# Five block ends of a two-layer float32 model: products of the first token half issued ahead, loads and remainders in other orders, and half-width increments in a triangular inverse

## The chip, the cores and the metric

The kernel runs on one core of one Trainium2 chip. The metric is the device time of one execution in microseconds (us), as the median of the runs. The profile is of one more execution; its times are us from its first instruction. Engines are written as the profile writes them: PE is the matrix engine (PEld its weight loads), DVE the vector engine, ACT the scalar engine, POOL GpSimd, SP the queue that issues the DMAs.

## What is computed

The reference is one block of a conformer kind, then two blocks with a memory attention each, all on 256 tokens of width 1024 in float32:

```
x = first_block(x, c, ...)          # conformer convolution, then conv_ffn (D_FF 2816)
for layer in (0, 1):
    x = layer_norm(ALPHA * x + 0.5 * swiglu(x, ffn1...))
    # layer 0: rwkv7_mix, a recurrence over tokens; layer 1: stick_breaking_mix
    x = layer_norm(ALPHA * x + mixer(x @ w_in) @ w_out)
    x = layer_norm(ALPHA * x + 0.5 * swiglu(x, ffn2...))
```

The recurrence is `state = state * w_t - (state kk_t) b_t^T + v_t k_t^T`, with a 64 x 64 state for each of 12 heads. The kernel solves it by chunks of 64 tokens, which needs the inverse of a triangular 64 x 64 matrix for each head and chunk.

## The kernel before

**Products.** Every matrix is held as two parts of type float32r, a rounded one (index 0, "hi") and the remainder (index 1, "lo"), and a product is three matmuls, hi x hi, hi x lo and lo x hi (`mm3`, lines 145 to 147). Tokens stand on the moving side: `actT[:, part, k, :]` holds the transposed activations, 8 tiles k of 128 features by 256 tokens. A weight tile of 128 x 128 is stationary. `FIRST` is the token half 0 to 127, `SECOND` the half 128 to 255.

**Weights.** Chunks of weights arrive by DMA in two raw buffers in turn (`Ring.load`, issued in order on SP). ACT rounds a chunk (`split_hi`), DVE or POOL makes the remainder (`split_lo`), and PE waits for `lo_done`. A raw buffer is loaded again only when `lo_done` has counted the remainder of the chunk in it, and a pair of parts is written again only when PE has used it.

**Order.** Each engine's order is written out by hand, stage after stage; the semaphores alone order the engines among each other. The stages are `ffn_stage` for the first block's FFN (`conv=True`) and four more, `rwkv_stages` (projections) and `rwkv_core`, and `stick_stages`.

**A block's end.** The last products of a stage are done by token half and column half (`BLOCKS`). `norm_dve_side` and `norm_act_side` normalize half 0 while PE works on half 1. PE turns half 0 (`turn_tokens(pe, hand, 0)`), and ACT and DVE make its hi and lo parts: `token_hi[0]` counts the six tiles of ACT, `token_lo[0]` first DVE's two tiles. `keep_busy(n)` issues n matmuls of the identity with itself, in plain float32, whose results nobody reads. After the last products come `keep_busy(pe, 14)`, and in the next stage the turning of half 1, `keep_busy(pe, 4)`, and `first_products`: for every k the two products of the hi tokens, then for every k the lo tokens' product (line 474). It has two outputs (gate and up) in the three FFN stages that follow a normalization, and one in `rwkv_stages` and `stick_stages`. That makes five such starts. `tokens_act` and `tokens_dve` make the parts of half 1; `pair_hi` counts the tiles 0, 1 and 2, 3 that DVE rounds, `token_hi[1]` the tiles 4 to 7 of ACT.

**The inverse.** `rwkv_core` does two rounds (T = 0, 1), each for two chunks and two groups p of six heads. It starts from a block diagonal of width 2, and level l (1 to 5) doubles the blocks. `squares` is 12 matmuls of 64 x 64 x 64 in plain float32, 6 heads by 2 chunks. A level computes Z = M D, the increments D Z and Z D^T into banks 2 + p and 4 + p, and DVE adds each whole bank to `Dm` or `DT` (lines 2652 and 2655).

Of the kernel before, what the change touches and what calls it, by code (L numbers as in the profile page):

```python
# [23 lines left out]
ALU = mybir.AluOpType  # L24
# [200 lines left out]
def build_program(nc, A, out):  # L225
    with ExitStack() as ctx:
# [179 lines left out]
        def tokens_dve(dve, i, t, yb, norm):  # L406

            w = slice(t * P, (t + 1) * P)
            dve.wait_ge(token_turned[t], 2 * i + 1)
# [7 lines left out]
            dve.wait_ge(token_hi[0], i + 1)  # L417
            first_lo(dve, yb, ACT_COLS).then_inc(token_lo[0], 1)
# [37 lines left out]
        def first_products(pe, i, outs, weights):  # L456

            for k in range(KD):
                if k == 0:
                    pe.wait_ge(token_hi[0], i + 1)  # L460
                    pe.wait_ge(token_lo[0], 2 * i + 2)
                    pe.wait_ge(pair_hi, 2 * i - 1)
                elif k == 2:
                    pe.wait_ge(pair_hi, 2 * i)
                elif k == 4:
                    pe.wait_ge(token_hi[1], i + 2)
                for n, out_ in enumerate(outs):
                    w = weights(n, k)
                    pe.matmul(out_, w[0], actT[:, 0, k], start=k == 0, stop=False)  # L469
                    pe.matmul(out_, w[1], actT[:, 0, k], start=False, stop=False)  # L470
            for k in range(KD):
                wait_tokens(pe, k, i)
                for n, out_ in enumerate(outs):
                    ins = pe.matmul(out_, weights(n, k)[0], actT[:, 1, k], start=False, stop=k == KD - 1)  # L474
            return ins

# [8 lines left out]
        FIRST = slice(0, P)  # L485
# [33 lines left out]
        SECOND = slice(P, 2 * P)  # L519
# [32 lines left out]
        def first_block():  # L552
# [135 lines left out]
            with nc.Block() as block:  # L688
                @block.sync
                def _(sp):  # L690
                    sp.dma_start(x_tok, A["x"][0].rearrange("(t p) d -> p t d", p=P)).then_inc(x_loaded, 16)
                    sp.dma_start(par[:, 0:n_first], A["par"][:, 0:n_first]).then_inc(params_loaded, 16)
                    for u in range(4):
                        for i in unit_chunks(u):
# [10 lines left out]
                    sp.dma_start(mem_raw.rearrange("p (k m) -> p k m", k=KD),  # L705
                                 A["mem_2"].rearrange("(k p) m -> p k m", p=P)).then_inc(mem_loaded, 16)
# [5 lines left out]
                    ring_a.load(sp, g_cols + 4)  # L712
                    sp.dma_start(rows[:, 0], A["norm_post_mix"][0].partition_broadcast(P)).then_inc(gates_loaded, 16)
# [3 lines left out]
                    load_mod(sp, 16)  # L717
                    load_mod(sp, 17)
# [549 lines left out]
        def ffn_stage(name, conv, norm, hand, next_a, next_b, take):  # L1268
# [202 lines left out]

            def up_first(pe):

                gate, up = ps[:, 4, 0:SEQ], up_of(0, 0)
                weights = lambda n, k: [a_parts[:, 0, s, n * BCH + k * P:n * BCH + (k + 1) * P] for s in range(2)]
                if conv:
                    ins = input_products(pe, gate, up, weights)
                else:
                    pe.wait_ge(ring_a.lo_done, sa + 1)
                    ins = first_products(pe, got, [gate, up], weights)  # L1480
                ins.then_inc(ring_a.used, 1)
# [375 lines left out]
        def rwkv_stages(take):  # L1857
# [88 lines left out]
            def _(pe):  # L1946
                def project(c):
# [6 lines left out]
                    if c == 0:  # L1954
                        first_products(pe, got, [chunk_bank(c)[:, 0]], lambda n, k: [
                            ring_a.part(g0, s, k * P, k * P + P) for s in range(2)]).then_inc(ring_a.used, 1)
                        return
# [12 lines left out]

                turn_tokens(pe, got, 1)
# [42 lines left out]
            def _(act):  # L2014
# [75 lines left out]
            def _(dve):  # L2090
# [84 lines left out]
        def rwkv_core(R, K, V, Q, BB, BON, CUM, KK, lowg, g_up, w_end, level_mask, pair_mask, below, upto, ident2,  # L2175
# [43 lines left out]
            def bank(b):  # L2219
                return ps[:, b, 0:H6 * HD].rearrange("p (m t) -> p m t", m=H6)  # L2220

# [81 lines left out]
            def _(pe):  # L2303
# [30 lines left out]

                for T in range(NT):
# [11 lines left out]
                    for l in LV:  # L2347
# [20 lines left out]
                        for p in range(2):  # L2368
# [213 lines left out]
            def _(dve):  # L2582
# [45 lines left out]
                for T in range(NT):  # L2628
# [19 lines left out]
                    for l in LV:  # L2648
                        for p in range(2):
                            if l < 5:  # L2650
                                dve.wait_ge(pe_out.sem, pe_out.at((("dD", l), T, p)))
                                dve.tensor_tensor(Dm[:, p], Dm[:, p], bank(2 + p), ALU.add)\
                                    .then_inc(dve_out.up((("D", l), T, p)), 1)
                            dve.wait_ge(pe_out.sem, pe_out.at((("dDT", l), T, p)))
                            dve.tensor_tensor(DT[:, p], DT[:, p], bank(4 + p), ALU.add)\
# [63 lines left out]
        def stick_stages(take, hand, got_norm):  # L2719
# [61 lines left out]
            def _(pe):  # L2781
                def project(c, n):
                    g = g0 + c
                    if c == 0 and n == 0:
                        return first_products(pe, got, [ps[:, bank(c), 0:SEQ]], lambda n, k: [
                            ring_a.part(g, s, k * 256, k * 256 + P) for s in range(2)])
# [80 lines left out]

                turn_tokens(pe, got, 1)
# [251 lines left out]
```

## Time and profile before

| what | value |
|---|---|
| median of 3 runs | 1456.42 us (1456.1 to 1458.33) |
| the profiled execution's own time | 1456.55 us |
| its span, first to last instruction | 1454.8 us |
| mean granted clock of PE in it | 0.998 of full speed |
| PE busy | 1414.5 us, 97% of the span |
| PEld busy | 1290.6 us, 89% |
| DVE busy | 952.5 us, 65% |
| ACT busy | 683.7 us, 47% |
| POOL busy | 156.9 us, 11% |

Matmuls overlap, and a row's duration holds the whole way through the array, so a matmul of 280 ns may follow another by less than half of that. What counts is the distance from start to start. A row of a timeline may stand for several instructions of one kind (x24): its length goes from the first one's start to the last one's end.

### The profile page before, as it was taken

The page shows a single profiled execution, that of the slowest core. Times are in us where ns is not written, and L with a number is a line of the kernel's source. Part 1 is how long each engine was busy: PE and PEld are TensorE (multiplying, and loading weights), DVE is VectorE, ACT ScalarE, POOL GpSimd, SP SyncE. Part 2 cuts the span into 40 slices and gives each one's busy share as a digit, 9 for nine tenths or more (in the row PEclk, how much of TensorE's full clock was granted, in tenths as well). Part 3 has the DMA queues.
Part 4 walks back from the last instruction along what each step waited for, and adds up shares of the span by engine and source line. Part 5 has one row for each costly group of instructions (what it writes and reads, how often), then busy time and mean ns, then how long its engine had stood idle before and what let it go on. Part 6 is the DMA issues. An engine that isn't in the chain of part 4 may idle for free.

```text
span 1454.8 us, 31311 instructions
## 1 busy us (share of the span) xinstructions
PE 1414.5 (97%) x12733; PEld 1290.6 (89%) x12733; DVE 952.5 (65%) x1290; ACT 683.7 (47%) x880; POOL 156.9 (11%) x182
## 2 busy tenths in 40 slices
PE   6999999999999999999989999999999999999997
PEld 5868799999999998988879999999999898899996
DVE  3657786667655556795786655675656778855656
ACT  5455654455433436743435433454334476534332
POOL 1442033221000004021300000000000011000000
PEclk9999999999999999999999999999999999999999
DMA  8975566666666645321036666566666344576662
GB/s 349 355 291 203 158 210 183 189 196 177 175 188 184 191 143 183 116 89 61 4 113 201 180 187 195 166 202 188 187 189 186 125 139 162 158 218 183 187 190 85
DMA packets 293910, 257.76 MB, mean 177 GB/s; under 512 B 7104, under 2 KB 270272, under 8 KB 290752
## 3 DMA queue, kind: packets, MB, share of 16 engines
q1 hardware_dynamic: 293824, 256.49, 57.5%
q8 instruction: 68, 1.11, 0.3%
q14 instruction: 18, 0.15, 0.0%
HBM read 255.42 MB, written 1.05 MB: 176 GB/s over the span
## 4 chain that ended last, share of the span: by engine, by line
PE 50%; DVE 4%; ACT 1%; issue 0%; DVEq 0%; ACTq 0%
PE ps L145 14%; PE ps L146 14%; PE ps L147 14%; PE ps L2331 3%; PE ps L383 1%; DVE stats L342 1%; DVE arena L340 1%; PE ps L390 1%; PE ps L469 0%; PE ps L474 0%; PE ps L470 0%; PE ps L2314 0%; PE ps L2322 0%; DVE gate_m L2634 0%; PE ps L2817 0%
## 5 line engine op out<-in xcount | busy, mean ns | idle before, releaser
L145 PE MATMUL ps<-actT,a_parts 128*128 128x256 f32 x2096 | 588.3, 281 | 2.9 <-DVE a_parts L130 2.0
L146 PE MATMUL ps<-actT,a_parts 128*128 128x256 f32 x2096 | 585.0, 279 | 0.0
L147 PE MATMUL ps<-actT,a_parts 128*128 128x256 f32 x2096 | 584.9, 279 | 0.0
L145 PEld LDWEIGHTS ps<-actT,a_parts 128*128 128x128 f32 x2096 | 394.0, 188 | 12.1 <-issue 3.8
L146 PEld LDWEIGHTS ps<-actT,a_parts 128*128 128x128 f32 x2096 | 393.8, 188 | 4.2
L147 PEld LDWEIGHTS ps<-actT,a_parts 128*128 128x128 f32 x2096 | 393.9, 188 | 0.0
L1350 DVE TENSOR_TENSOR a_parts<-a_raw,a_parts 128x2048 fp32r<-128x2048 f32 x100 | 238.4, 2384 | 54.5 <-ACT a_parts L1347 54.1
L1364 DVE TENSOR_TENSOR b_parts<-b_raw,b_parts 128x1024 fp32r<-128x1024 f32 x72 | 88.3, 1226 | 160.3 <-ACT b_parts L1361 160.3
L1347 ACT ACTIVATE a_parts<-a_raw 128x2048 fp32r<-128x2048 f32 x100 | 190.4, 1904 | 0.8 <-DMA a_raw<-in_ffn_w_up 0.8
L1361 ACT ACTIVATE b_parts<-b_raw 128x1024 fp32r<-128x1024 f32 x90 | 95.3, 1058 | 171.0 <-PE ps L147 171.0
L145 PE MATMUL ps<-b_parts,hid 128*128 128x512 f32 x400 | 158.1, 395 | 1.0 <-DVE hid L1461 1.0
L146 PE MATMUL ps<-b_parts,hid 128*128 128x512 f32 x400 | 158.3, 396 | 0.0
L147 PE MATMUL ps<-b_parts,hid 128*128 128x512 f32 x400 | 158.3, 396 | 0.0
L1409 ACT ACTIVATE arena<-ps 128x256 f32<-128x256 f32 x88 | 33.8, 385 | 241.6 <-PE ps L147 241.5
L130 DVE TENSOR_TENSOR a_parts<-a_raw,a_parts 128x2048 fp32r<-128x2048 f32 (+2 forms) x38 | 81.3, 2139 | 43.8 <-ACT a_parts L125 43.7
L147 PEld LDWEIGHTS ps<-b_parts,hid 128*128 128x128 f32 x400 | 75.1, 188 | 18.2
L1455 DVE TENSOR_TENSOR arena<-arena,ps 128x256 f32<-128x256 f32 x88 | 37.0, 421 | 81.3 <-ACT arena L1409 81.3
L145 PEld LDWEIGHTS ps<-b_parts,hid 128*128 128x128 f32 x400 | 75.1, 188 | 15.1 <-POOL b_parts L130 1.2
L146 PEld LDWEIGHTS ps<-b_parts,hid 128*128 128x128 f32 x400 | 75.1, 188 | 13.8
L125 ACT ACTIVATE a_parts<-a_raw 128x2048 fp32r<-128x2048 f32 (+2 forms) x43 | 77.0, 1791 | 14.7 <-DMA a_raw<-in_a_pw_w 11.8
L1364 POOL TENSOR_TENSOR b_parts<-b_raw,b_parts 128x1024 fp32r<-128x1024 f32 x18 | 45.9, 2547 | 107.6 <-ACT b_parts L1361 107.6
L1461 DVE TENSOR_TENSOR hid<-arena,hid 128x256 fp32r<-128x256 f32 x110 | 46.8, 426 | 3.8
(392 smaller groups left out, 1818.8 us busy)
## 6 DMA issues: line engine op xcount, KB each, us to landing
a_raw<-in_ffn_w_gate SPq DMA_DIRECT2D x88, 512.0 KB, 4.0
a_raw<-in_ffn_w_up SPq DMA_DIRECT2D x88, 512.0 KB, 5.2
b_raw<-in_ffn_w_down SPq DMA_DIRECT2D x88, 512.0 KB, 3.3
arena<-in_mod_w SPq DMA_DIRECT2D x24, 1024.0 KB, 10.1
a_raw<-in_f_up_w SPq DMA_DIRECT2D x44, 512.0 KB, 5.0
b_raw<-in_f_down_w SPq DMA_DIRECT2D x22, 512.0 KB, 3.3
a_raw<-in_rwkv_w_in SPq DMA_DIRECT2D x10, 1024.0 KB, 5.3
a_raw<-in_sb_w_in SPq DMA_DIRECT2D x10, 1024.0 KB, 5.1
```

The lines of the kernel that those rows point to most:

```text
L125: act.activation(self.parts[:, g % 2, 0, w], self.raw[:, g % 2, w], ACT.Copy).then_inc(self.hi_done, 1)
L130: dve.tensor_tensor(self.parts[:, g % 2, 1, w], self.raw[:, g % 2, w], self.parts[:, g % 2, 0, w].bitcast(F32), ALU.subtract).then_inc(sel ...
L145: pe.matmul(out, lhs[0], rhs[0], start=start, stop=False)
L146: pe.matmul(out, lhs[0], rhs[1], start=False, stop=False)
L147: return pe.matmul(out, lhs[1], rhs[0], start=False, stop=stop)
L1347: act.activation(a_parts[:, q, 0], a_raw[:, q], ACT.Copy).then_inc(ring_a.hi_done, 1)
L1350: dve.tensor_tensor(a_parts[:, q, 1], a_raw[:, q], a_parts[:, q, 0].bitcast(F32), ALU.subtract).then_inc(ring_a.lo_done, 1)
L1361: act.activation(b_of(q, j)[:, 0], b_raw[:, q], ACT.Copy).then_inc(ring_b.hi_done, 1)
L1364: lo.tensor_tensor(b_of(q, j)[:, 1], b_raw[:, q], b_of(q, j)[:, 0].bitcast(F32), ALU.subtract).then_inc(ring_b.lo_done, 1)
L1455: dve.tensor_tensor(hf[:, q], cg[:, q], up, ALU.mult).then_inc(f_step, 1)
L1461: dve.tensor_tensor(h_of(q, j)[:, 1], hf[:, q], h_of(q, j)[:, 0].bitcast(F32), ALU.subtract).then_inc(h_done, 1)
L2331: ins = pe.matmul(bank(b)[half[c], mm], lhs[half[c], p, mm], rhs[half[c], p, mm], start=True, stop=True)
```

## The change

1. `first_ahead` is new. It issues the hi tokens' two products of half `FIRST` alone for one output, 16 matmuls with 128 moving columns. It stands ahead of `turn_tokens(pe, got, 1)` for the one output of `rwkv_stages` and `stick_stages` (the change's own title speaks of four block ends; the code has five such starts), and in the FFN stages for the gate ahead of the turning and for the up projection behind it, in place of `keep_busy(pe, 4)`. `first_products` then does only `SECOND` for the hi tokens; its lo tokens' products stay 256 wide. `tokens_dve` makes the lo part of half 0's six tiles before it waits for the turned half 1.
2. Four orders: the load of `mem_2` in the first block goes behind the 17th chunk of `mod_w`, and chunks 17 and 18 go ahead of four loads of rows; POOL's second remainder at the start of the first FFN waits for DVE's remainder of a weight chunk; ACT rounds chunk 2 of the recurrent stage ahead of `take_out(0)`; DVE makes the remainders of chunks 1 and 2 ahead of the `k_a` and `mu` columns and of `mix(0)`.
3. In the inverse, `one_side` computes 32 of the 64 columns of each increment (those of the even blocks for `Dm`, of the odd ones for `DT`; the others are zero) into a packed bank, and DVE adds 192 elements in place of 384.

```diff
@@ tokens_dve
+            dve.wait_ge(token_hi[0], i + 1)
+            first_lo(dve, yb, ACT_COLS).then_inc(token_lo[0], 1)
             dve.wait_ge(token_turned[t], 2 * i + 1)
...
-            dve.wait_ge(token_hi[0], i + 1)
-            first_lo(dve, yb, ACT_COLS).then_inc(token_lo[0], 1)
@@ first_products
-                    pe.wait_ge(token_hi[0], i + 1)
-                    pe.wait_ge(token_lo[0], 2 * i + 2)
...
-                    pe.matmul(out_, w[0], actT[:, 0, k], start=k == 0, stop=False)
-                    pe.matmul(out_, w[1], actT[:, 0, k], start=False, stop=False)
+                    for part in w:
+                        pe.matmul(out_[:, SECOND], part, actT[:, 0, k, SECOND], start=False, stop=False,
+                                  skip_group_check=True)
...
+        def first_ahead(pe, i, n, out_, weights):
+
+            for k in range(KD):
+                if k == 0:
+                    pe.wait_ge(token_hi[0], i + 1)
+                    pe.wait_ge(token_lo[0], 2 * i + 2)
+                for s, part in enumerate(weights(n, k)):
+                    pe.matmul(out_[:, FIRST], part, actT[:, 0, k, FIRST], start=k == 0 and s == 0, stop=False,
+                              skip_group_check=True)
@@ first block, SP
-                    sp.dma_start(mem_raw.rearrange("p (k m) -> p k m", k=KD),
-                                 A["mem_2"].rearrange("(k p) m -> p k m", p=P)).then_inc(mem_loaded, 16)
                     load_mod(sp, 12)
...
                     ring_a.load(sp, g_cols + 4)
+                    load_mod(sp, 16)
+                    sp.dma_start(mem_raw.rearrange("p (k m) -> p k m", k=KD),
+                                 A["mem_2"].rearrange("(k p) m -> p k m", p=P)).then_inc(mem_loaded, 16)
+                    load_mod(sp, 17)
...
-                    load_mod(sp, 16)
-                    load_mod(sp, 17)
@@ ffn_stage, PE
-                if take is not None:
+                if take is not None and got_norm is not None:
+                    pe.wait_ge(ring_a.lo_done, sa + 1)
+                    first_ahead(pe, got, 0, first_outs[0], first_weights)
                     turn_tokens(pe, got, 1)
-                    keep_busy(pe, 4 if got_norm is not None else 5)
+                    first_ahead(pe, got, 1, first_outs[1], first_weights)
+                elif take is not None:
+                    turn_tokens(pe, got, 1)
+                    keep_busy(pe, 5)
@@ ffn_stage, POOL, first FFN only
                     ring_b.split_lo(pool, gb)
+                    pool.wait_ge(ring_a.lo_done, ga + 3)
                     ring_b.split_lo(pool, gb + 1)
@@ rwkv_stages, PE; in stick_stages the output is ps[:, bank(0), 0:SEQ]
+                ring_a.wait_split(pe, g0)
+                first_ahead(pe, got, 0, chunk_bank(0)[:, 0], first_weights)
                 turn_tokens(pe, got, 1)
                 keep_busy(pe, 4)
@@ rwkv_stages, ACT
                 next_hi(1)
+                next_hi(2)
                 act.wait_ge(dve_out.sem, dve_out.at("mu"))
                 take_out(0)
-                next_hi(2)
@@ rwkv_stages, DVE
                 take[1](dve)
+                next_lo(1)
...
-                next_lo(1)
+                next_lo(2)
                 mix(0)
-                next_lo(2)
                 mix(1)
@@ rwkv_core
+            def side(ap, l, odd):
+                return ap.rearrange("q (g two w) -> q g two w", two=2, w=1 << l)[:, :, odd]
...
+                def one_side(p, b, lhs, rhs, l, odd):
+                    for mm in range(H6):
+                        out_ = packed_bank(b)[:, mm * HD // 2:(mm + 1) * HD // 2]
+                        for c in range(2):
+                            ins = pe.matmul(packed(out_[half[c]], l), lhs[half[c], p, mm],
+                                            side(rhs[half[c], p, mm], l, odd), start=True, stop=True)
+                    return ins
...
-                                squares(p, 2 + p, DT, Z).then_inc(pe_out.up((("dD", l), T, p)), 1)
-                            squares(p, 4 + p, Z, DT).then_inc(pe_out.up((("dDT", l), T, p)), 1)
+                                one_side(p, 2 + p, DT, Z, l, 0).then_inc(pe_out.up((("dD", l), T, p)), 1)
+                            one_side(p, 4 + p, Z, DT, l, 1).then_inc(pe_out.up((("dDT", l), T, p)), 1)
...
-                                dve.tensor_tensor(Dm[:, p], Dm[:, p], bank(2 + p), ALU.add)\
+                                even = side(all_heads(Dm[:, p]), l, 0)
+                                dve.tensor_tensor(even, even, packed(packed_bank(2 + p), l), ALU.add)\
```

## Rows read from the trace of the kernel before

**Rows 1.** The core's span and mean granted PE clock.
```profile
core 0: 1454.8 us, clock 0.998
```

**Rows 2.** PE's waits over the whole span: us in total, times, longest.
```profile
PE ps L619 <- DMA arena<-in_mod_w: 2.2, 2, 1.2
...
PE ps L145 <- DVE a_parts L130: 2.0, 3, 1.2
...
PE ps L2380 <- DVE gate_f L2655: 1.5, 2, 0.8
...
PE ps L145 <- DVE hid L1461: 1.0, 1, 1.0
...
PE ps L2331 <- DVE gate_m L2652: 0.7, 1, 0.7
...
PE ps L2308 <- DVE arena L2604: 0.5, 1, 0.5
```

**Rows 3.** PE's timeline where `("ffn1", 1)` starts: start, us, engine, line.
```profile
954.02 3.29 PE L383 MATMUL ps<-ident 128*128 128x128 f32 x28
957.14 1.06 PE L390 MATMUL ps<-ident,x_tok 128*128 128x128 f32 x8
...
962.82 2.03 PE L474 MATMUL ps<-actT,a_parts 128*128 128x256 f32 x16
964.69 0.28 PE L145 MATMUL ps<-actT,a_parts 128*128 128x256 f32 x1
```

**Rows 4.** Timeline of ACT and DVE at the same place.
```profile
955.07 0.84 ACT L499 ACTIVATE actT<-arena 128x768 fp32r<-128x768 f32 x1
...
955.80 0.37 DVE L490 TENSOR_TENSOR actT<-arena,actT 128x256 fp32r<-128x256 f32 x1
...
959.54 0.29 DVE L416 CAST actT<-arena 128x256 fp32r<-128x256 f32 x1
...
959.78 0.63 ACT L404 ACTIVATE actT<-arena 128x512 fp32r<-128x512 f32 x1
```

**Rows 5.** PEld's timeline in `rwkv_stages`, around 24 matmuls with 2 moving columns.
```profile
594.37 2.76 PEld L1988 LDWEIGHTS ps<-head_ones,arena 128*128 128x128 f32 x24
597.05 0.19 PEld L145 LDWEIGHTS ps<-actT,a_parts 128*128 128x128 f32 x1
```

**Rows 6.** PEld's group of the token transposes: busy, mean ns.
```profile
L390 PEld LDWEIGHTS ps<-ident,x_tok 128*128 128x128 f32 x96 | 10.3, 141 | 5.3 <-DVE x_tok L365 4.5 <-DVE x_tok L1724 0.6
```

**Rows 7.** Timelines of ACT and PE at the start of `rwkv_stages`.
```profile
558.18 0.63 ACT L404 ACTIVATE actT<-arena 128x512 fp32r<-128x512 f32 x1
...
561.26 0.47 ACT L2022 ACTIVATE arena<-ps,small 128x256 f32<-128x256 f32 x1 [1.49 <-PE ps L474]
...
561.71 0.39 PE L145 MATMUL ps<-actT,a_parts 128*128 128x256 f32 x1 [0.55 <-DVE a_parts L130]
...
565.95 0.39 PE L145 MATMUL ps<-actT,a_parts 128*128 128x256 f32 x1 [1.17 <-DVE a_parts L130]
```

**Rows 8.** PE's timeline at the start of `stick_stages`.
```profile
1152.61 1.25 PE L474 MATMUL ps<-actT,a_parts 128*128 128x256 f32 x8
```

**Rows 9.** PE's timeline in a level of the inverse, then two DVE groups by shape.
```profile
664.86 1.57 PE L2331 MATMUL ps<-gate_m,arena 64*64 64x64 f32 x48
...
L2655 DVE TENSOR_TENSOR gate_f<-gate_f,ps 128x384 f32<-128x384 f32 x20 | 11.1, 553 | 8.0 <-PE ps L2331 6.0
...
L1455 DVE TENSOR_TENSOR arena<-arena,ps 128x256 f32<-128x256 f32 x88 | 37.0, 421 | 81.3 <-ACT arena L1409 81.3
```

**Rows 10.** Timelines of POOL and DVE at the start of the first FFN.
```profile
181.72 4.99 POOL L130 TENSOR_TENSOR b_parts<-b_raw,b_parts 128x1024 fp32r<-128x1024 f32 x2 [62.86 <-DVE a_parts L1387]
...
184.49 2.38 DVE L1459 CAST hid<-arena 128x256 fp32r<-128x256 f32 x1
```

**Rows 11.** Timelines of SP and ACT in the first block, `mem_2`'s load and first reader.
```profile
52.90 4.07 SPq L705 DMA_DIRECT2D b_raw<-in_mem  x1
...
102.37 1.90 ACT L853 ACTIVATE b_parts<-b_raw 128x2048 fp32r<-128x2048 f32 x1
```

More of the change, by code:

```diff
@@ L473, in first_products @@
                 for n, out_ in enumerate(outs):
-                    ins = pe.matmul(out_, weights(n, k)[0], actT[:, 1, k], start=False, stop=k == KD - 1)
-            return ins
+                    ins = pe.matmul(out_, weights(n, k)[0], actT[:, 1, k], start=False, stop=k == KD - 1,
+                                    skip_group_check=True)
+            return ins
+        def first_ahead(pe, i, n, out_, weights):
[5 more added lines that the diff above has]
+                    pe.matmul(out_[:, FIRST], part, actT[:, 0, k, FIRST], start=k == 0 and s == 0, stop=False,
+                              skip_group_check=True)
         def first_affine(eng, i, yb, norm, ks, scaled):
@@ L483, in first_affine @@
             return ins
-        FIRST = slice(0, P)
+        FIRST, SECOND = slice(0, P), slice(P, 2 * P)
         ACT_COLS, DVE_COLS = slice(0, 6), slice(6, KD)
@@ L1470, in up_of, with first_weights @@
                 return ps[:, 1, SEQ:2 * SEQ] if kicked(q, j) else ps[:, 4 + q, SEQ:2 * SEQ]
+            first_outs = [ps[:, 4, 0:SEQ], up_of(0, 0)]
+            def first_weights(n, k):
+                return [a_parts[:, 0, s, n * BCH + k * P:n * BCH + (k + 1) * P] for s in range(2)]
             def up_first(pe):
-                gate, up = ps[:, 4, 0:SEQ], up_of(0, 0)
-                weights = lambda n, k: [a_parts[:, 0, s, n * BCH + k * P:n * BCH + (k + 1) * P] for s in range(2)]
                 if conv:
-                    ins = input_products(pe, gate, up, weights)
+                    ins = input_products(pe, *first_outs, first_weights)
                 else:
-                    pe.wait_ge(ring_a.lo_done, sa + 1)
-                    ins = first_products(pe, got, [gate, up], weights)
+                    ins = first_products(pe, got, first_outs, first_weights)
                 ins.then_inc(ring_a.used, 1)
@@ L1954, in project @@
                     if c == 0:
-                        first_products(pe, got, [chunk_bank(c)[:, 0]], lambda n, k: [
-                            ring_a.part(g0, s, k * P, k * P + P) for s in range(2)]).then_inc(ring_a.used, 1)
+                        first_products(pe, got, [chunk_bank(c)[:, 0]], first_weights).then_inc(ring_a.used, 1)
                         return
@@ L1969, in low_rank, with first_weights @@
                     ins.then_inc(norm_pe.up(name), 1)
+                def first_weights(n, k):
+                    return [ring_a.part(g0, s, k * P, k * P + P) for s in range(2)]
+                ring_a.wait_split(pe, g0)
+                first_ahead(pe, got, 0, chunk_bank(0)[:, 0], first_weights)
                 turn_tokens(pe, got, 1)
@@ L2220, in bank, with packed, all_heads, packed_bank @@
                 return ps[:, b, 0:H6 * HD].rearrange("p (m t) -> p m t", m=H6)
+            def side(ap, l, odd):
+                return ap.rearrange("q (g two w) -> q g two w", two=2, w=1 << l)[:, :, odd]
+            def packed(ap, l):
+                return ap.rearrange("q (g w) -> q g w", w=1 << l)
+            def all_heads(ap):
+                return ap.rearrange("q m t -> q (m t)")
+            def packed_bank(b):
+                return ps[:, b, 0:H6 * HD // 2]
             def bmask(m):
@@ L2784, in project @@
                     if c == 0 and n == 0:
-                        return first_products(pe, got, [ps[:, bank(c), 0:SEQ]], lambda n, k: [
-                            ring_a.part(g, s, k * 256, k * 256 + P) for s in range(2)])
+                        return first_products(pe, got, [ps[:, bank(c), 0:SEQ]], first_weights)
                     for k in range(KD):
@@ L2866, in behind, with first_weights @@
                         turn(4)
+                def first_weights(n, k):
+                    return [ring_a.part(g0, s, k * 256, k * 256 + P) for s in range(2)]
+                ring_a.wait_split(pe, g0)
+                first_ahead(pe, got, 0, ps[:, bank(0), 0:SEQ], first_weights)
                 turn_tokens(pe, got, 1)
```

4 lines of the change are left out of this document (2 added, 2 removed).

## The prediction

> **What bounds the kernel.** I read the cores view first: a span of 1454.8 us at a mean granted clock of 0.998 [rows 1], so nothing here is about the clock. The profiled execution took 1456.55 us, 1.75 around its span and 0.13 above the median of the three runs, and the sum is made against 1456.55. Then the page: PE is busy for 97% of the span, so a change gains where it takes matmuls from PE or ends one of PE's waits. The waits view says how little there is of the second kind [rows 2]: 2.0 us for remainders made by DVE, 1.5 and 0.7 and 0.5 us in the inverse, 1.0 us for `hid`. Last come the timelines at the edited places, where the distances from start to start tell what a matmul costs.
>
> **Products of half 0 ahead.** In the FFN stage of [rows 3] PE turns half 1 at 957.14, does `keep_busy(4)`, 32 hi products and 16 lo products of 256 columns, and begins the next tile at 964.69. That is 8 transposes, 8 instructions of `keep_busy` and 48 products, 64 slots in 7.55 us: 0.117 each (the 16 of line 474 take 1.87 us, 0.117 each). `keep_busy(14)` keeps its place, so PE is free for the new products at 957.14 and no sooner. What they wait for is then there: ACT's six tiles are done at 955.91 and DVE's lo tiles at 956.17 [rows 4].
>
> The new order counts: 16 half products, 8 transposes, 16 half products, 32 half products of `SECOND`, 16 lo products 256 wide. 32 full products and 8 fillers go, 64 half ones come. With h for a half product the stretch takes 64 h + 24 x 0.117 = 64 h + 2.80, against 64 x 0.117 = 7.47. All hangs on h, and no float32r matmul of the trace moves fewer than 256 columns. The nearest row is line 1988: 24 matmuls with 128 x 128 weights and only 2 moving columns. Their loads begin at 594.37 and the next load at 597.05 [rows 5], so each takes 0.112 us though almost nothing moves. The weight load sets the pace. A half product loads the same 128 x 128 weights as a whole one, and the change loads every hi and lo weight tile twice. I take h = 0.112, with 0.117 (the whole product's) above.
>
> Nothing behind it is late. With h = 0.112 the turning moves 1.8 us later, DVE's second pair from 959.83 to 961.6 and ACT's four tiles from 960.41 to 962.2 [rows 4]. PE would begin `SECOND` at 957.14 + 1.79 + 0.93 + 1.79 = 961.65 and want k = 4 at 963.4. The lo part of half 0's six tiles, moved ahead of DVE's wait, runs in the time in which DVE waits for the later turning. So each of the three FFN starts costs 7.15 + 2.80 - 7.47 = +2.5 us, together **+7.5** (+7.0 at 0.109, +8.4 at 0.117).
>
> The Trainium skill speaks for another h here. "TensorE: Matmul & The Clock Gate", section "Back-to-back issue gap", gives about 81 ns for a matmul with its weight load at 128 columns. By it the three starts would cost 3 x (64 x 0.081 + 2.80 - 7.47) = +1.5 us. The row of line 1988 shows 112 ns for the load alone, so I leave the rule among the rivals.
>
> In `rwkv_stages` one output gets 16 half products ahead, 1.79 us, and its 16 hi products become half ones. ACT's tiles come at 558.81 + 1.79 = 560.60 [rows 7] and hold k = 4. Then 8 half and 8 whole products end at 562.45, 1.6 us after 560.85 (561.26 less the 0.41 in which ACT sees it). The next chunk's rounding, at 561.63 behind `take_out(0)`, now goes first: it starts at about 562.85, 1.2 later. PE waited for that chunk's remainder until 565.95 and will wait until 567.15: **+1.2** (0.9 to 1.4). The order of ACT and DVE is thus worth the 0.4 us that it takes off 1.6. `take_out(0)`, `mix(0)` and the tanh behind them come some 2 us later, hidden by the 5.6 us of the third chunk's products; without that cover the low-rank products would be late by it.
>
> In `stick_stages` ACT's tiles hold k = 4 too. Before, the 8 lo products began at 1152.61 [rows 8]; ACT's tiles move by 1.79, and half products save 0.1 to 0.2 of it behind k = 4: **+1.6** (1.4 to 1.9). Five starts: 7.5 + 1.2 + 1.6 = +10.3.
>
> **The inverse.** 48 instructions of `squares` take 1.57 us less one matmul's 0.22 from first to last start, 0.029 each, so 24 (12 matmuls of two passes) 0.70 [rows 9]. Two chunks run side by side, so a pair takes 0.058, half of 0.117 with half of the 128 weight columns. The weights stay 64 x 64. By the proportion of lines 1988 and 145, 0.112 to 0.117, the pair falls to 0.056. There are 4 + 5 calls for two groups and two rounds, 36 of them, with 12 pairs each: 432 x 0.0025 = -1.1. The other bound is that the moving columns set the pace: -432 x 0.029 = -12.5. Above, nothing.
>
> DVE's additions hide behind PE, except at four places: two waits for the last `DT`, one for `Dm` at level 1 of round 1, one behind `DT` ahead of the normalization [rows 2]. An addition of 384 elements takes 0.553 and one of 256 takes 0.421 [rows 9], so 192 take 0.355, 0.2 less: -0.8. The stepped access has no row. Every addition but these four has PE's 0.7 us a call as cover, so a slower one costs at most that 0.8. Together **-1.9** (0 to -13.3).
>
> **POOL at the first FFN.** POOL makes two remainders in one stretch, 181.72 to 186.71, and a cast of DVE that begins in it, 128 x 256, takes 2.38 us [rows 10] where the same shape elsewhere takes 0.29 [rows 4]. It ends with POOL's. PE waits 1.0 us for `hid` behind it [rows 2]. With the second remainder held until DVE's chunk, the cast is done in 0.3 us and the wait goes: **-1.0** (0 to -1.1). The held remainder starts about 188. PE wants it only after the first remainder's products and another tile's, and SP's load behind it, some 1 us later than now, is for the tile after that.
>
> **Loads in the first block.** PE waits for a load twice and only for `mod_w` [rows 2], both times ahead of the moved ones. `mem_2` is issued at 52.90 and first read at 102.37 [rows 11]. SP now stops at chunk 17 of `mod_w`, until PE has used a slot, ahead of `mem_2` and the four rows. PE uses that slot in the products of the third of eight tiles, and `mem_2` is read in the fifth and the rows from the fifth on. **0** (-0.5 to +0.5).
>
> **Sum.** 1456.55 + 10.3 - 1.9 - 1.0 = 1463.95, say **1464.0 us**, 0.5% slower.
>
> **Rivals.** *Half products cost by their columns.* Line 390's loads of 128 columns take 141 ns where others take 188 [rows 6], so a load need not take 112. If h falls to 0.058, an FFN stretch is 64 x 0.058 + 2.80 - 7.47 = -1.0, given back in part by a wait of about 0.5 for ACT's four tiles: -1.4 over three, 0.2 for the other two starts. The time is 1456.55 - 1.2 - 1.9 - 1.0 = 1452.4, faster. All terms balance at 256 h - 18.5 = 2.9, h = 0.084. Against it stand 24 loads at 0.112. In between, at h = 0.081, I get +3.3 - 2.9, 1456.9. That h is the figure of the Trainium skill's section above.
>
> *The increments pay by their columns.* -12.5 for -1.1 in the inverse gives 1452.6, faster too. For it: 64 columns in two passes and 64 weight columns could each be the limit of a pair. Against it the same row of 2 columns.
>
> *A narrow float32r product runs as a plain float32 one.* `keep_busy(14)` is 28 instructions in 3.12 us [rows 3]: a plain product of 128 columns costs two, 0.23. Then 256 h - 18.5 = +41, 1494.7. For it: no narrow one stands in the trace. Against it: nothing does but that float32r is one instruction wherever it stands.
>
> *The orders of loads do more than hold.* A late row or a late `mem_2` would stop PE near 102 us; 1 to 5 us more, 1466 to 1469.
>
> **Chances.** The forecast's case 0.64. Half products by columns or nearly so 0.12, half of it below 1453.5. Increments by columns 0.07. Plain float32 pace 0.11. Loads late 0.03; another mix, near no change, 0.03. A measurement of this kernel tells about 0.2%, 2.9 us, from no change. Below 1453.5 lie 0.06 + 0.06; within lie the rest of the second rival, and a twelfth of the first case where the inverse gives back 5 or more: 0.15; slower 0.73. The range that leaves out the plain pace and the fastest ends is 1455 to 1468.
>
> **What would show it.** In the changed kernel's timeline, `first_ahead` has 16 products in 1.8 us and `SECOND` the same pace as before; the next tile of the `("ffn1", 1)` start begins 10.0 us after the end of `keep_busy(14)`. The x24 rows of the increments still lie 0.67 to 0.70 apart, DVE's additions take 0.36, and the cast at the first FFN takes 0.29 with PE's wait for `hid` gone. The prediction is wrong if the new products lie 0.06 or 0.23 apart, or if the increments' calls shrink to 0.4 us.

## The result, and the profile after

The changed kernel takes 1466.17 us (median of 6 runs, 1464.62 to 1467.32). The kernel before, run beside it, takes 1458.34 (6 runs, 1456.1 to 1458.78). The ratio is 1.0058, 95% interval [1.0048, 1.0069]: slower by 0.6%. The prediction said 1464.0, slower by 0.5%, range 1455 to 1468.

The profiled execution of the changed kernel has a span of 1463.7 us, 8.9 more than [rows 1]. The cores view of it:

```profile
core 0: 1463.7 us, clock 0.998
```

PE's timeline at the start of `("ffn1", 1)`, answering [rows 3] (`first_ahead` is line 484, `SECOND` 468, the lo products 473):

```profile
956.66 3.29 PE L383 MATMUL ps<-ident 128*128 128x128 f32 x28
959.70 1.98 PE L484 MATMUL ps<-actT,a_parts 128*128 128x128 f32 x16
961.52 1.06 PE L390 MATMUL ps<-ident,x_tok 128*128 128x128 f32 x8
962.34 1.98 PE L484 MATMUL ps<-actT,a_parts 128*128 128x128 f32 x16
964.15 3.74 PE L468 MATMUL ps<-actT,a_parts 128*128 128x128 f32 x32
967.73 2.10 PE L473 MATMUL ps<-actT,a_parts 128*128 128x256 f32 x16
969.67 0.28 PE L145 MATMUL ps<-actT,a_parts 128*128 128x256 f32 x1
```

From start to start the half products take (961.52 - 959.70) / 16 = 0.114 us ahead, with the hand-over to the turning in it, and 3.58 / 32 = 0.112 in `SECOND`. A whole product took 0.117 [rows 3]. Half the columns save 4% of the time. No wait stands between the rows: PE is full from 956.66 to 969.67, 13.01 us. Before, the same stretch ran from 954.02 to 964.69 [rows 3], 10.67. The difference is +2.34.

DVE there, answering [rows 4]:

```profile
959.61 0.95 DVE L500 TENSOR_TENSOR actT<-arena,actT 128x768 fp32r<-128x768 f32 x1
962.18 0.73 DVE L415 TENSOR_SCALAR arena<-ps,par 128x128 f32<-128x128 f32 x2 [1.62 <-PE ps L390]
962.95 0.29 DVE L418 CAST actT<-arena 128x256 fp32r<-128x256 f32 x1
```

The moved lo part ends at 960.56, inside the time in which DVE waits for the later turning. The first pair is there at 963.24 (962.95 + 0.29), 0.9 us before PE wants it for `SECOND` at 964.15.

The start of `rwkv_stages`, answering [rows 7], and of `stick_stages`, answering [rows 8]:

```profile
559.16 1.69 PE L468 MATMUL ps<-actT,a_parts 128*128 128x128 f32 x12 [0.24 <-DVE actT L418]
...
566.23 0.39 PE L145 MATMUL ps<-actT,a_parts 128*128 128x256 f32 x1 [1.21 <-DVE a_parts L130]
```
```profile
1157.73 1.68 PE L468 MATMUL ps<-actT,a_parts 128*128 128x128 f32 x12 [0.24 <-DVE actT L418]
```

With one output and not two, PE waits 0.24 us for DVE's pair, a wait that the prediction didn't name. It is hardly new: the kernel before waits 0.17 us for the same pair, at 558.29 and at 1150.98. The second chunk's remainder lets PE go on at 566.23, where it did at 565.95 [rows 7]; but by then the kernel is 0.86 us ahead of the old one (the gain in the first FFN, below), so this start costs 0.28 + 0.86 = +1.1.

The inverse, answering [rows 9]. Two neighbouring rows of PE's timeline, then DVE's additions by shape between 640 and 740 us:

```profile
662.58 0.87 PE L2373 MATMUL ps<-gate_f,arena 64*64 64x32 f32 x24
663.28 0.87 PE L2373 MATMUL ps<-arena,gate_f 64*64 64x32 f32 x24
```
```profile
L2699 DVE TENSOR_TENSOR gate_f<-gate_f,ps 128x192 f32<-128x192 f32 x20 | 7.1, 353 | 11.4 <-PE ps L2373 11.4
L2695 DVE TENSOR_TENSOR gate_m<-gate_m,ps 128x192 f32<-128x192 f32 x16 | 5.6, 352 | 12.9 <-PE ps L2373 12.9
```

24 instructions of 32 moving columns still lie 0.70 us apart: PE gains nothing by the missing columns. DVE's additions fell from 0.553 to 0.353, and the stepped access costs nothing. PE's waits, answering [rows 2]:

```profile
PE ps L2355 <- issue: 2.3, 3, 1.5
...
PE ps L2422 <- DVE gate_f L2699: 1.1, 2, 0.6
...
PE ps L2364 <- DVE gate_m L2695: 0.5, 1, 0.5
...
PE ps L2341 <- DVE arena L2646: 0.3, 1, 0.3
```

Three of the inverse's waits are 0.8 us shorter in all, and the one for `hid` (1.0 before) is gone. New is 2.3 us of "issue", in which PE waited for nothing that the profile shows; the kernel before had 0.4 on that line. The longest, 1.5 us near 646, is in the profiles of all four kernels that have the products ahead (1.2 to 1.6) and of none without. It costs next to nothing: in the others PE waits 0.9 us right behind that place, for the DVE operation that is line 2634 in the kernel before, and in these four that wait is gone.

DVE and POOL at the first FFN, answering [rows 10]:

```profile
184.37 0.30 DVE L1468 CAST hid<-arena 128x256 fp32r<-128x256 f32 x1
...
191.14 2.59 DVE L1470 TENSOR_TENSOR hid<-arena,hid 128x256 fp32r<-128x256 f32 x1
```
```profile
188.09 2.41 POOL L130 TENSOR_TENSOR b_parts<-b_raw,b_parts 128x1024 fp32r<-128x1024 f32 x1 [4.12 <-DVE a_parts L1359]
191.05 2.40 POOL L1373 TENSOR_TENSOR b_parts<-b_raw,b_parts 128x1024 fp32r<-128x1024 f32 x1 [0.55 <-ACT b_parts L1370]
```

The cast fell from 2.38 to 0.30 us. The collision isn't gone, only moved: a remainder of DVE, 0.43 elsewhere, now takes 2.59 beside POOL's at 191.05, where PE doesn't wait for it. In both kernels the held instruction ends 0.2 to 0.3 us behind POOL's (186.87 and 186.71, 193.73 and 193.45). The Trainium skill has the rule, on its page "SBUF — State Buffer", section "Who interferes with whom": a cast in DVE's two-port mode, or a `tensor_tensor` with both inputs in SBUF, shares a port pair with GpSimd, and whoever comes second is held for the other's whole instruction. The two held durations agree with it; that the cast runs in the two-port mode, no row shows.

Holding POOL's remainder back has a price that the prediction put at nothing. SP issues its loads in order, and the load of `b_raw` that waits for this remainder is now issued at 190.68, not 186.89. The two loads of `a_raw` behind it are late by 2.0 us. First the row of the kernel before, then those of the changed kernel:

```profile
189.71 1.00 SPq L1318 DMA_DIRECT2D a_raw<-in_f_up_w  x2
```
```profile
191.70 1.00 SPq L1327 DMA_DIRECT2D a_raw<-in_f_up_w  x2
192.56 1.92 ACT L1356 ACTIVATE a_parts<-a_raw 128x2048 fp32r<-128x2048 f32 x1 [1.59 <-DMA a_raw<-in_f_up_w]
206.15 0.38 PE L145 MATMUL ps<-actT,a_parts 128*128 128x256 f32 x1 [0.21 <-DVE a_parts L1359]
```

ACT waits 1.59 us for that load, its rounding and then DVE's remainders come later, and PE waits 0.21 us where it did not wait before. From start to start the early `hid` gains 1.2 us, and 0.4 to 0.5 of it is lost again here. Six profiles have POOL's new wait. In two of them ACT waits 0.76 and 1.06 us for this load and PE not at all; in four ACT waits 1.56, 1.59, 1.61 and 1.86 and PE 0.17, 0.21, 0.23 and 0.50. Why the load lands sooner in some is open.

### The profile page after: what moved, and what is told of

It reads as the page before. It is cut to its first block, busy times and chain, and to the rows that moved or that the text cites. A ratio compares the mean times of both kernels' runs of the same rounds, so it can differ in the third digit from the quotient of the medians.

```text
span 1463.7 us, 31520 instructions
## 1 busy us (share of the span) xinstructions
PE 1426.0 (97%) x12837; PEld 1302.4 (89%) x12837; DVE 945.6 (65%) x1290; ACT 683.4 (47%) x880; POOL 156.7 (11%) x182
## 4 chain that ended last, share of the span: by engine, by line
PE 51%; DVE 4%; issue 1%; ACT 0%; DVEq 0%; ACTq 0%
PE ps L145 14%; PE ps L146 14%; PE ps L147 14%; PE ps L2373 2%; PE ps L2364 1%; PE ps L383 1%; PE ps L468 1%; PE ps L484 1%; DVE stats L342 1%; DVE arena L340 1%; PE ps L390 1%; PE ps L2355 0%; PE ps L473 0%; PE ps L2347 0%; PE ps L2860 0%
```

## Where the clock fell

The totals of two profiles can't be compared to 1 us here until one thing is taken out. At one place in `rwkv_stages` and at one at the end of the recurrence's round 1 the granted clock falls to 0.50 (1.2 GHz) for 3 to 4 us in some profiles and not in others, with the same instructions. Two windows tables of PE (stretch, its length, PE busy, instructions, clock, DMA share and GB/s), first of the kernel with only the new order of loads, then of the one with only the narrow increments:

```profile
597.00:598.00 1.00, 1.00 (x11) 0.99 1.09 388
598.00:599.00 1.00, 1.00 (x7) 0.50 0.93 312
599.00:600.00 1.00, 1.00 (x7) 0.50 0.00 0
```
```profile
597.00:598.00 1.00, 1.00 (x10) 1.00 1.10 392
598.00:600.00 2.00, 2.00 (x20) 1.00 0.37 124
```

What PE did just before is the same in both: 24 matmuls that move 2 columns each, 2.7 us. The second place comes behind 64 x 64 products with a wait of 1.34 us between them, and the changed kernel's own profile has it:

```profile
732.00:734.00 2.00, 1.41 (x35) 0.79 1.15 350
734.00:736.00 2.00, 2.00 (x41) 0.50 0.73 289
```

Cut at five landmarks of PE's timeline, all profiles become comparable. Columns: from `keep_busy(14)` at the start of `rwkv_stages` to the 24 two-column matmuls; on to the memory scores; on to the 12 products with `g_up` in round 1; on to the second turning for the norm; the last four columns are from one turning of half 0 to the next across the starts of `ffn2`/0, `ffn1`/1, `stick_stages`, and the last start with what lies behind it to the span's end. * is a stretch in which the clock fell.

```
                 start   scores   inverse  end of   start of  start of  start of  last start
                 rwkv                      round 1  ffn2,0    ffn1,1    stick     to end
before           42.06   16.71    113.77   19.03    191.10    191.08    110.92    201.1
changed          43.31   16.71    113.04   19.63*   193.47    193.46    112.39    203.5
inverse only     42.15   16.71    112.45   19.92*   191.08    191.08    110.93    201.1
no ahead         41.77   16.71    112.40   19.87*   191.21    191.09    110.84    201.1
ahead only       43.72   18.27*   113.79   19.62*   193.47    193.47    112.39    203.5
pool only        42.17   18.21*   114.03   19.00    191.09    191.09    110.92    201.1
gate behind      42.17   18.25*   114.10   19.82*   191.75    191.74    110.77    201.8
rwkv order only  41.78   18.24*   113.73   19.01    191.09    191.18    110.87    201.2
loads only       42.17   18.25*   114.02   18.98    191.09    191.09    110.86    201.2
```

The first fall costs 1.54 us (18.25 less 16.71), the second 0.6 to 0.9. The profile of before has neither, and its execution is 1.8 us below the median (1456.55 against 1458.34). The Trainium skill ("TensorE: Matmul & The Clock Gate", section "Seeing it yourself") calls clock events in a trace not fully reliable; here the instruction counts agree with them, 7 matmuls to the microsecond in place of 10 or 11.

## The experiments

Each kernel below is the kernel before with the edit named, unless it says otherwise. Ratios are to the kernel before on the same chip.

**The parts by themselves.** Four kernels: (1) only `one_side` and its additions; (2) all of the change but the products ahead; (3) only the products ahead, with `first_lo` moved; (4) only POOL's wait. The core of (2) against the changed kernel:

```diff
-                if take is not None and got_norm is not None:
-                    pe.wait_ge(ring_a.lo_done, sa + 1)
-                    first_ahead(pe, got, 0, first_outs[0], first_weights)
+                if take is not None:
                     turn_tokens(pe, got, 1)
-                    first_ahead(pe, got, 1, first_outs[1], first_weights)
-                elif take is not None:
-                    turn_tokens(pe, got, 1)
-                    keep_busy(pe, 5)
+                    keep_busy(pe, 4 if got_norm is not None else 5)
```

(1) 

> The kernel before with only the narrow increments of the inverse. My theory, with what the trace after has shown: the pairs keep their 0.058 us, so PE gains nothing per call; DVE's shorter additions end four waits sooner, worth 0.5 to 1.9 us in all: 0.9987 to 1.0 of before. Rival, pay by moving columns: 12 us less (0.992). Rival, the change costs here: stepped access or new waits on DVE make it 1 us or more slower.

(2) 

> The changed kernel without its products ahead at the block ends: inverse, POOL's wait, the orders of loads and the rwkv orders stay. My theory: the products ahead are the whole loss, so this is 1.5 to 3.5 us faster than before (0.9976 to 0.999) and some 10 us faster than the changed kernel. Rival, the cost is shared or sits in the orders: no faster than before.

(3) 

> The kernel before with only the products ahead at the five starts. My theory: 64 half products at 0.112 us in each FFN start, 2.5 us each, 1.6 in rwkv_stages (where its old orders stay) and 1.6 in stick_stages: +10 to +11 us, 1.007 of before. Rival, half products pay by columns: -1 us, 0.999. Rival, plain float32 pace: +41 us, 1.028.

(4) 

> The kernel before with only POOL's wait ahead of its second remainder. My theory: the cast takes 0.3 us in place of 2.4 and PE's 1 us wait for hid goes: 0.7 to 1.1 us less, 0.9993 of before, at the edge of what the measurement tells; its trace shows the wait gone. Rival: the remainder, moved later, blocks another operation that PE waits for, and the time is the same or more.

```
                 median    ratio    95% interval       span of the profile
inverse only     1457.18   0.9995   [0.9987, 1.0004]   1454.5
no ahead         1455.44   0.9989   [0.9980, 0.9998]   1452.8
ahead only       1467.18   1.0066   [1.0053, 1.0079]   1467.0
pool only        1457.07   1.0000   [0.9991, 1.0008]   1456.2
```

The products ahead are the whole loss: alone they cost 0.66%, and without them the rest is faster than before. (1) and (4) are too small for the timing; the traces carry them. In the table above the inverse stretch is 113.73 to 114.10 with wide increments and 112.40 or 112.45 in (1) and (2): 1.3 to 1.7 us gained. In (4) PE's wait for `hid` is gone, and from its wait at 175 us to the turning at 360 it needs 0.75 us less than before: 1.2 gained, and 0.4 lost again where it waits 0.17 us for DVE's remainder at 206.56, as the changed kernel does. So the rival stated for (4), that another operation comes late, is true in part. In (2) that wait is missing, and the same stretch takes 1.3 us less. The rival that the half products pay by columns would have made (3) 0.999.

**How many slots, or how late?** The products ahead do two things: more matmuls and a later turning. Call a slot the place of one matmul instruction on PE; a start has 64 before. This kernel separates them. It has half products for the gate alone, at the three FFN starts alone, and behind the turning where the fillers were:

```diff
-                if take is not None:
+                if take is not None and got_norm is not None:
                     turn_tokens(pe, got, 1)
-                    keep_busy(pe, 4 if got_norm is not None else 5)
+                    pe.wait_ge(ring_a.lo_done, sa + 1)
+                    first_ahead(pe, got, 0, first_outs[0], first_weights)
+                elif take is not None:
+                    turn_tokens(pe, got, 1)
+                    keep_busy(pe, 5)
```

> The kernel before with the half products of the gate alone, at the three FFN starts alone, and behind the turning in place of the four fillers, so that nothing is turned later. PE then has 8 transposes, 32 half and 32 whole products where it had 64 slots. My theory, cost by count: 32 x 0.112 + 40 x 0.117 - 7.47 = +0.8 us each, +2.4 in all (1.0016). Rival, cost by columns: -0.9 each, -2.8 in all (0.998). Rival, the loss comes from the later turning and not from the count: no change or better.

1459.11 us, ratio 1.0014 [1.0005, 1.0023]; by the table 0.66 us for each start (191.75 less 191.09), 2.0 in all. Its timeline:

```profile
960.38 1.06 PE L390 MATMUL ps<-ident,x_tok 128*128 128x128 f32 x8
961.20 1.98 PE L490 MATMUL ps<-actT,a_parts 128*128 128x128 f32 x16
963.01 0.39 PE L471 MATMUL ps<-actT,a_parts 128*128 128x128 f32 x2
```

Nothing waits and nothing is turned later, and still the start costs 0.66 us (+0.8 was expected), about what 8 more slots cost: 72 in place of 64. The count is the cause. In the changed kernel a start has 88 slots in 9.97 us, 0.113 each, which leaves nothing for the lateness. The rivals (-2.8 by columns, nothing by lateness) fall.

**The orders by themselves.** Only `next_hi(2)`, `next_lo(1)` and `next_lo(2)` moved forward:

> The kernel before with only the new orders of ACT and DVE at the start of rwkv_stages. My theory: PE waits 0.55 and 1.17 us there for remainders, and the second chunk's rounding and remainder, now first, could save up to about 1 us of it: 0 to -1 us (0.9993 to 1.0). Rival: take_out, moved behind, makes the low-rank products late, +1 us or more.

1457.45, ratio 0.9995 [0.9986, 1.0004]. Its start of `rwkv_stages` takes 41.78 us, the unedited kernels' 42.06 to 42.17: 0.3 to 0.4 less. With the products ahead and the old orders it takes 43.72, with both 43.31: the orders are worth 0.4 there too. Only the new order of loads:

> The kernel before with only the new order of loads in the first block. My theory: no wait of PE ends sooner or later by it but those for mod_w, 0 within 0.5 us (1.0). Rival: mem_2 or the rows come late and PE stops, +1 to +5 us.

1458.2, ratio 1.0003 [0.9994, 1.0012]. `keep_busy(14)` of `rwkv_stages` starts at 552.55, before at 552.42: nothing, as expected.

**What sets the pace of a narrow product?** Trains of 16 behind PE's last product of the changed kernel:

```diff
+                    for k in range(16):
+                        pe.matmul(ps[:, 4, 0:192], wt[k], mv[:, 0:192], start=True, stop=True)
+                    for k in range(16):
+                        pe.matmul(ps[:, 4, 0:128], wt[k], mv[:, 0:128], start=True, stop=True)
```

> The changed kernel with eleven trains of 16 independent matmuls behind PE's last product of the last stage; they write a bank nobody reads, and the output is untouched. Moving columns 512, 256, 192, 128, 64 and 2 in float32r with 128 x 128 weights; 128 and 256 with 64 weight columns; plain float32 with 64 x 64 weights and 64, 32 and 128 moving columns. My theory: with 128 weight columns the pace is a floor of 0.109 to 0.112 us from 192 columns down to 2, and grows with the columns only from 256 on (0.117, 0.23 at 512); with 64 weight columns the floor halves to about 0.056. Rival, columns: 0.117 falls to 0.058 at 128. Rival, a floor per instruction that doesn't depend on the weights' width: 64 weight columns take 0.11 too. The span may grow by up to 8 us through the trains themselves.

```profile
1458.02 3.81 PE L1589 MATMUL ps<-a_parts 128*128 128x512 f32 x16
1461.66 2.08 PE L1591 MATMUL ps<-a_parts 128*128 128x256 f32 x16
1463.58 1.93 PE L1593 MATMUL ps<-a_parts 128*128 128x192 f32 x16
1465.35 1.92 PE L1595 MATMUL ps<-a_parts 128*128 128x128 f32 x16
1467.10 1.92 PE L1597 MATMUL ps<-a_parts 128*128 128x64 f32 x16
1468.86 2.83 PE L1599 MATMUL ps<-a_parts 128*128 128x2 f32 x16
...
1476.71 2.07 PE L1605 MATMUL ps<-ident 64*64 64x64 f32 x32
1478.62 2.00 PE L1607 MATMUL ps<-ident 64*64 64x32 f32 x32
1480.46 3.68 PE L1609 MATMUL ps<-ident 64*64 64x128 f32 x32
```

Start to start over 16: 0.228 at 512 moving columns, 0.120 at 256, 0.111 at 192, 0.109 at 128, 0.110 at 64. In the train of 2 columns the clock fell to 0.50 until about 1476, so that train and the two behind it, not shown, say nothing of full speed. The last three lie behind the fall, at a clock of 1.00. They are plain float32 products with the 64 x 64 weights of the inverse, two instructions each: 0.060 an instruction with 64 moving columns, 0.058 with 32, some 0.11 with 128. So halving the increments' columns had nothing to give, here too. The second kernel puts 16 products of 512 columns ahead of each train:

> The trains again, because in the first look the granted clock fell to 0.5 over the narrowest and over those with 64 weight columns. Now a train of 16 with 512 moving columns stands ahead of each: float32r with 128 weight columns and 128 and 2 moving; 64 weight columns and 256, 128, 64, 32 moving; 32 weight columns and 64 moving; plain float32 64 x 64 with 64 and 32 moving. They write banks nobody reads. My theory: at a granted clock of 1.0 the floor follows the weight columns: 0.109 at 128, about 0.056 at 64, less at 32, and 0.117 and 0.058 for 256 and 128 moving with 64 weight columns. Rival: the floor of a float32r product is 0.109 whatever its weights' width. The span grows by some 60 us through the trains themselves.

```profile
1459.26 1.90 PE L1593 MATMUL ps<-a_parts 128*128 128x128 f32 x16
1460.99 3.90 PE L1590 MATMUL ps<-a_parts 128*128 128x512 f32 x16
1464.73 1.84 PE L1596 MATMUL ps<-a_parts 128*128 128x2 f32 x16
1466.43 3.93 PE L1590 MATMUL ps<-a_parts 128*128 128x512 f32 x16
1470.20 1.99 PE L1599 MATMUL ps<-a_parts 128*64 128x256 f32 x16
1472.02 3.81 PE L1590 MATMUL ps<-a_parts 128*128 128x512 f32 x16
1475.68 1.12 PE L1602 MATMUL ps<-a_parts 128*64 128x128 f32 x16
1476.63 3.88 PE L1590 MATMUL ps<-a_parts 128*128 128x512 f32 x16
1480.36 1.07 PE L1605 MATMUL ps<-a_parts 128*64 128x64 f32 x16
...
1489.62 0.67 PE L1611 MATMUL ps<-a_parts 128*32 128x64 f32 x16
```

The clock stayed at 1.00. 128 weight columns: 0.108 with 128 moving, 0.106 with 2. 64 weight columns: 0.114 with 256 moving, 0.059 with 128, 0.056 with 64, 0.057 with 32. 32 weight columns: 0.032 with 64. So in these trains a product costs the larger of two times, one that goes with its moving columns and one that goes with its weight columns, and at 128 moving columns on 128 of weights only the second is left. (The trains lengthened the spans by 20.7 and 38.4 us, not by the 8 and 60 expected.) The rival of one floor for all widths would have shown 0.109 with 64 weight columns.

**Can the falls of the clock be had back?** Two kernels. In the first only the 12 sums with `head_ones` changed, to move 128 columns of which the two are read:

```diff
-                        ins = pe.matmul(ps[:, 4, at:at + 2], BON[:, m, t * P:(t + 1) * P], head_ones[:, 0:P:HD],
-                                        start=True, stop=True)
+                        ins = pe.matmul(ps[:, 4, at:at + P].rearrange("p (w h) -> p w h", h=2),
+                                        BON[:, m, t * P:(t + 1) * P],
+                                        head_ones[:].rearrange("p (h w) -> p w h", h=2), start=True, stop=True)
```

> The kernel before with one line changed: the 12 products with head_ones in rwkv_stages (24 instructions) move 128 columns, not 2; only the two that were there before are read. In five profiles of other kernels the granted clock fell to 0.5 for 3.4 us right behind those 24 and the stretch took 1.5 us longer; in the others, with the same instructions there, it did not. My theory: 128 columns cost what 2 do (0.11), and the clock no longer falls there: the profile shows 16.7 us from them to the next landmark, and the median falls by what share of executions had the dip, 0.5 to 1.5 us (0.999 to 0.9997). Rival: the fall has nothing to do with the narrow products, and the time is the same or, if they are slower, up to 1.3 us more.

1458.09, ratio 1.0003 [0.9993, 1.0012]: no gain. The clock did not fall there in its profile, nor in the next kernel's, but the stretch takes 17.31 us in place of 16.71: the stepped columns cost 0.13 each, not 0.11, 0.6 in all. Of 11 profiles with two columns 7 have the fall; two profiles without it don't prove a cure. Its 11 runs lie between 1457.64 and 1459.03, the 21 of before beside it between 1456.13 and 1460.77. The second has the parts of "no ahead", these sums, and 5 and 2 unread products of `ident` in the waits of 1.3 and 0.5 us at the end of round 1:

> The changed kernel without its products ahead, with the wide sums of e10 and with 5 and 2 unread products of the identity in two waits of PE at the end of round 1 (1.3 and 0.5 us), behind which the clock fell in some profiles. My theory: e2 was 0.9989 of before; without the two dips (1.5 and 0.6 to 0.9 us where they come) it is 0.9975 to 0.9985, some 3 us faster than before and 11 faster than the changed kernel. Rival: the dips are not influenced by this, 0.9989 again.

1455.89, ratio 0.9986 [0.9977, 0.9995]. The end of round 1 takes 19.04, without a fall; but its profile has one between 176 and 184 us, where none of those in the table has. Expected was 0.9975 to 0.9985. Against "no ahead" (0.9989) nothing is told apart: what the wide sums and the fillers are worth stays open. Either is some 2 us faster than before and 10 faster than the changed kernel. The simpler one, the change without its products ahead, is the version to keep.

## Why the prediction was right

- **The start of an FFN: right.** 64 half products at 0.112 were put at +2.5 for each start, 7.5 in all. Measured: +2.34 in the timeline, +2.4 by the table, 7.1 in all. From the end of `keep_busy(14)` to the next tile it is 9.97 us (10.0 forecast). About half of the 0.4 too much is a reading: the stretch before is 7.55 us by its rows and went into the sum as 7.47. The step that carried the forecast was to read the price of a float32r product from 24 plain ones of two columns, 0.112: the trains show 0.108 for a float32r product of 128 columns and 0.106 for one of 2.
- **`rwkv_stages` and `stick_stages`: right.** +1.2 and +1.6 forecast, +1.1 to +1.25 (43.31 less 42.17 or 42.06) and +1.5 measured, with a wait of 0.24 us in each that was not forecast and was 0.17 before. The orders' 0.4 is confirmed with and without the products ahead.
- **The inverse: right in sign, too large.** -1.9 forecast. That DVE's additions end four waits sooner was right; that each pair of products gets 0.0025 us cheaper was not. The seven profiles with wide increments and no other fall of the clock in the stretch have a mean of 113.92 there; the narrow ones have 112.45, 112.40, 112.39 (the last kernel), 112.50 (the changed kernel with the second trains) and 113.04 (the changed kernel): 1.4 less on the mean, and 0.7 in the pair of profiles that the result rests on. The changed kernel with the first trains has 114.05, with a third fall of the clock inside the stretch, at 701.67, and is left out. The term that failed is the pairs' -1.1: a call still takes 0.70 us, and the trains show 64 weight columns at 0.056 to 0.057 however few move. DVE's -0.8 came, and about half a microsecond more, which no single wait shows. The 1.5 us of "issue" come with the products ahead, but why more instructions elsewhere should hold PE there is open. They are given back: the 112.50 contains such a stop of 1.2 us. Why the changed kernel's own profile has only 113.04 stays open too.
- **POOL: right in sign, one step wrong.** -1.0 forecast, -0.7 measured. The wait for `hid` went, worth 1.2 us from start to start. The step that failed was the loads behind it: the prediction had SP's load "some 1 us later" and without effect. The load of `b_raw` came 3.8 us later, those of `a_raw` 2.0 later, and PE waits 0.21 us at 206.15, which costs 0.4 to 0.5. The collision with POOL came back too (2.59 us), but it is not in this path: DVE is done with it at 193.73 and then waits 0.78 us for ACT.
- **Loads: right**, 0 within 0.2 us.
- **The sum.** Forecast +7.4 on 1456.55. The medians differ by 7.8, the spans by 8.9, of which 0.6 is the fallen clock. Piece by piece between the two profiles: 7.15 (FFN starts) + 1.25 + 1.47 - 0.73 (inverse) - 0.86 (all up to 552 us) + 0.60 (clock) = 8.88. Some of the nearness is luck, since errors cancel: the FFN starts were put 0.4 too dear, the inverse 0.5 to 1.2 and POOL 0.3 too generous. That the forecast in microseconds is 2.2 low is mostly its base: the execution profiled was 1.8 below the median measured beside the changed kernel.
- **The rivals.** Half products by columns would have given 1452.4; trains and starts show 0.108 to 0.114. Increments by columns: no call shrank. A narrow float32r product at the plain pace: not seen. Late loads: not seen. The 0.081 us of the Trainium skill ("TensorE: Matmul & The Clock Gate", section "Back-to-back issue gap"), which gave 1456.9, isn't confirmed. (The prediction's own 256 h - 18.5 is +2.2 at that h, not +3.3, so 1455.9; no conclusion hangs on it.) Another section of that page of the Trainium skill, "LDWEIGHTS (loading the stationary operand)", has a load cost its columns over 1.2 GHz, an estimate of 107, 53 and 27 ns for 128, 64 and 32. The narrowest trains, at 106, 56 and 32, agree at 128, nearly at 64, and lie a fifth above at 32.

## What to carry to other kernels

Splitting a product along its moving side loads the same weights twice, so before cutting one, compare its moving columns with twice its weight columns: for float32r here 256 moving columns on 128 of weights are the point of balance, and cutting them in two nearly doubles the cost. Work can be pulled into an idle slot of PE only if it isn't made longer by the cut; the eight filler slots of a start (0.94 us) pay, by count, for eight extra products; the gate alone needs sixteen, gate and up thirty-two. An operation held back to free one engine can also hold back a load that waits for it, and with it every load behind that one in the same queue: look at the queue's timeline too. When effects of 1 us matter, compare stretches between landmarks over several profiles and look at the granted clock of each stretch first.

## Not expected of the hardware

- The clock falls to 1.2 GHz while PE is busy 100% of the time, 2.4 to 3.9 us after the first of 24 matmuls with 2 moving columns (2.7 us of them): in 7 of 11 profiles, 1.54 us lost each time. That these matmuls are the cause isn't shown. It is run to run, not by kernel: two kernels that reach these matmuls at 594.58 and 594.59 differ in it.
- A fetch of 128 moving columns in steps of 64 made a plain product take 0.13 us where 2 columns or 128 contiguous ones take 0.11.
- A remainder of DVE that meets POOL's is held for 2.2 us (2.59 for 0.43), the same as the cast was.
